# A new order of the seven products in a channel mixer's tiles, with PSUM banks of its own for the third product, on one NeuronCore

## The reference

```python
def causal_dwconv(u, prev, w, b):
    full = jnp.concatenate([prev, u], axis=1)
    return b + sum(full[:, i:i + L] * w[i] for i in range(3)), full[:, -2:]

def conv_glu(h, prev, w_in, conv_w, conv_b, w_out):
    g, u = jnp.split(h @ w_in, [2816], axis=-1)
    gc, new_prev = causal_dwconv(g, prev, conv_w, conv_b)
    return (jax.nn.gelu(gc, approximate=False) * u) @ w_out, new_prev
```

## Time and profile before

| | |
|---|---|
| median of 3 runs | 2664.94 us (2663.79 to 2665.84) |
| the profiled execution: time | 2669.07 us |
| its span in the trace | 2667.2 us |
| mean granted clock of TensorE | 0.991 |
| TensorE busy | 2586.1 us, 97% |
| VectorE busy | 1485.7 us, 56% |
| ScalarE busy | 1001.2 us, 38% |
| GpSimd busy | 991.4 us, 37% |
| DMA queues, share of 16 engines' span | 24.3% (SyncE's and ScalarE's loads and stores) |
| channel mixer of layer 0, tiles 1 to 21 | 599.2 to 1047.0 us |
| tile 1 of layer 1 | from 1954.9 us |

### The profile page before, as it was taken

One profiled execution on the slowest core, in us unless ns is written; L12 is line 12 of the kernel. 1 busy time (PEld: TensorE's weight loads), 2 busy tenths in 40 slices (PEclk: granted clock), 3 DMA queues, 4 the chain that ended last, 5 costly groups with the idle time before them and its releaser, 6 DMA issues.

```text
span 2667.2 us, 43368 instructions
## 1 busy us (share of the span) xinstructions
PE 2586.1 (97%) x18206; PEld 2502.4 (94%) x18206; DVE 1485.7 (56%) x2646; ACT 1001.2 (38%) x1651; POOL 991.4 (37%) x560
## 2 busy tenths in 40 slices
PE   8999999997999999999999989999979999999999
PEld 6899999997999999999998988889979999999999
DVE  6635353477545545555625875555685455545554
ACT  6333333363322332111437766444543323331111
POOL 5121212165443344443522223223373443444431
PEclk9999999998999999999999999999989999999999
DMA  3111111122222224222213354122112222233222
GB/s 109 34 36 34 36 38 36 35 97 65 87 73 81 80 81 178 80 97 97 70 40 119 116 193 134 51 88 73 60 62 89 73 80 73 88 117 134 97 97 99
DMA packets 182158, 221.93 MB, mean 83 GB/s; under 512 B 16689, under 2 KB 145343, under 8 KB 181327
## 3 DMA queue, kind: packets, MB, share of 16 engines
q1 hardware_dynamic: 179567, 217.08, 24.3%
q10 hardware_dynamic: 2400, 2.10, 0.3%
HBM read 160.56 MB, written 58.59 MB: 82 GB/s over the span
## 4 chain that ended last, share of the span: by engine, by line
PE 85%; DVE 9%; issue 2%; ACT 2%; DMA 1%; SPq 0%; POOL 0%; DVEq 0%; ACTq 0%; POOLq 0%
PE ps L341 13%; PE ps L343 13%; PE ps L342 13%; PE ps L751 10%; PE ps L753 10%; PE ps L752 10%; PE ps L2285 3%; PE ps L1214 1%; PE ps L2269 1%; PE ps L1201 1%; PE ps L1202 1%; PE ps L1203 1%; PE ps L1285 1%; DVE hflat L486 1%; DVE xT L585 1%
## 5 line engine op out<-in xcount | busy, mean ns | idle before, releaser
L585 DVE TENSOR_TENSOR xT<-xT,ps 128x352 f32<-128x352 f32 x672 | 347.2, 519 | 249.4 <-PE ps L343 248.2
L1084 POOL TENSOR_TENSOR wlo<-wraw,whi 128x1024 fp32r<-128x1024 f32 x84 | 211.4, 2516 | 475.4 <-DVE s_raw L963 475.4
L306 POOL TENSOR_TENSOR wlo<-wraw,whi 128x2048 fp32r<-128x2048 f32 (+1 forms) x37 | 168.4, 4552 | 500.8 <-ACT whi L299 471.4
L341 PE MATMUL ps<-fahi,whi 128*128 128x352 f32 x960 | 311.1, 324 | 0.1
L343 PE MATMUL ps<-fahi,wlo 128*128 128x352 f32 x960 | 308.3, 321 | 0.0
L342 PE MATMUL ps<-falo,whi 128*128 128x352 f32 x960 | 307.9, 321 | 0.0
L299 ACT ACTIVATE whi<-wraw 128x2048 fp32r<-128x2048 f32 x40 | 76.6, 1915 | 401.9 <-DMA wraw<-w_ffn_out 332.4
L341 PE MATMUL ps<-hh,whi 128*128 128x352 f32 x648 | 213.6, 330 | 0.6 <-ACT cqr L2598 0.3
L343 PE MATMUL ps<-hh,wlo 128*128 128x352 f32 x648 | 208.0, 321 | 0.0
L342 PE MATMUL ps<-hl,whi 128*128 128x352 f32 x648 | 207.8, 321 | 0.0
L753 PE MATMUL ps<-hh,wlo 128*128 128x264 f32 x672 | 191.2, 284 | 0.0
(11 more groups left out here) (411 smaller groups left out, 8061.4 us busy)
## 6 DMA issues: line engine op xcount, KB each, us to landing
wraw<-w_ffn_in SPq DMA_DIRECT2D x88, 512.0 KB, 3.8
s_a<-hf SPq DMA_DIRECT2D x44, 528.0 KB, 3.4
wraw<-w_ffn_out SPq DMA_DIRECT2D x44, 512.0 KB, 4.3
fa<-s_a SPq DMA_DIRECT2D x40, 528.0 KB, 6.1
wraw<-w_gla_in SPq DMA_DIRECT2D x24, 512.0 KB, 4.7
s_x<-xT SPq DMA_DIRECT2D x6, 1408.0 KB, 5.8
xback<-s_x SPq DMA_DIRECT2D x4, 2112.0 KB, 12.9
s_k<-kw SPq DMA_DIRECT2D x8, 784.0 KB, 3.3
```

Source lines behind the costliest of these rows:

```text
L306: pool.tensor_tensor(lo[:, 0:cols], raw[:, 0:cols], hi[:, 0:cols].bitcast(F32), ALU.subtract).then_inc(S("w_lo"), 1)
L341: nc.tensor.matmul(out, w[0], x[0], start=start, stop=False)
L585: dve.tensor_tensor(xT[:, m, tc(j)], xT[:, m, tc(j)], ps[:, banks[i % len(banks)], 0:TC], ALU.add)\
L1084: return pool.tensor_tensor(lo[:, cols], raw[:, cols], hi[:, cols].bitcast(F32), ALU.subtract)
```

## The change

The products run in the order P1, P2, P3, P6, P5, P7, P4. P3 (the product of X22) no longer gathers with P5 but has banks 2 and 3 (`U_EARLY`), and `gate_right` adds it to the right gate by an addition of its own, after the fifth product (P5). The convolution of a tile follows in that tile, ahead of `up_right` and `up_left`; `glu(f)` follows these. P4, in banks 0 and 1, is now the last product, so that the next tile's P2 waits for `up_left`. In the first two or three tiles the order is an own one. T1 and T3 are formed in another way from the same blocks. In tile 1 all low parts are made on VectorE; GpSimd starts with the extra weights of tile 2. Its three calls per tile are now `w_low_in`, `w_low_extra` (512 and 1024 columns) and `w_low_side`. On SyncE the second half of a tile's weights is loaded after the seventh product instead of the sixth, and in the last tile the reloads of the residual stream (`xback`) and of the first activations stand in another order.

```diff
-        U_SUM, U_DOWN, U_SIDE = 6, 0, 4
+        U_SUM, U_DOWN, U_SIDE, U_EARLY = 6, 0, 4, 2
+        ORDER = ("P1", "P2", "P3", "P6", "P5", "P7", "P4")
...
+            def p2():
+                if f == 1:
+                    pe.wait_ge(S("gate_taken"), 2 * layer + 1)
+                else:
+                    pe.wait_ge(S("summed"), nth("summed", 4 * u))
+                product(U_DOWN, w_in(1), x_part(HK, 0)).then_inc(S("prod"), 1)
...
+            def p3():
+                pe.wait_ge(S("s_lo"), nth("s_lo", 3 * u + 2))
+                if f == 1:
+                    pe.wait_ge(S("gate_taken"), 2 * layer + 2)
+                else:
+                    pe.wait_ge(S("summed"), nth("summed", 4 * u - 2))
+                product(U_EARLY, w_extra(2), x_part(HK, TH)).then_inc(S("prod"), 1)
...
act_ffn:
+            snap(1, 1)
+            w_hi_sums(2)
+            snap(1, 2)
+            for f in range(2, NF):
+                snap(f, 0)
+                if f < 4:
+                    gelu((0, 2)[f - 2])
...
                 snap(f, 1)
                 if f < NF - 1:
                     w_hi_sums(f + 1)
                 else:
                     a_high(0)
                 snap(f, 2)
-            gelu(NF - 1)
+                gelu(1 if f == 2 else f)
...
dve_ffn:
+            def up_left(f):
+                u, left = unit_no(layer, f), two_of(a_rows(f)[:, 0, :])
+                dve.wait_ge(S("prod"), nth("prod", 7 * u + ORDER.index("P4") + 1))
+                dve.wait_ge(S("summed"), nth("summed", 4 * u + 3))
+                dve.tensor_tensor(left, left, two(U_DOWN), ALU.add).then_inc(S("summed"), 1)
+            def gate_right(f):
+                u, v = unit_no(layer, f), two_of(fg[f % 2][:, 2 + TH:2 + T])
+                dve.wait_ge(S("snap"), nth("snap", 3 * u + 2))
+                dve.wait_ge(S("prod"), nth("prod", 7 * u + ORDER.index("P5") + 1))
+                dve.tensor_tensor(v, v, two(U_EARLY), ALU.add).then_inc(S("early"), 1)
+                dve.wait_ge(S("early"), nth("early", u + 1))
                 dve.tensor_tensor(v, v, two(U_SIDE), ALU.add).then_inc(S("summed"), 1)
...
             s_sums(1)
-            t_sums()
+            t_sum("T1")
+            t_sum("T2")
+            w_low_in(1)
+            w_low_extra(1)
+            t_sum("T3")
+            t_sum("T4")
             t_low("T2", 2)
+            w_low_side(1)
+            t_low("T1", 1)
+            t_low("T3", 3)
             gate_left(1)
-            conv(0)
             t_low("T4", 4)
             s_sums(2)
+            w_low_in(2)
+            gate_right(1)
+            up_right(1)
+            up_left(1)
+            conv(0)
+            gate_left(2)
+            s_sums(3)
             glu(0)
-            the_rest(1)
             conv(1)
-            for f in range(2, NF):
+            gate_right(2)
+            up_right(2)
+            glu(1)
+            up_left(2)
+            conv(2)
+            gate_left(3)
+            s_sums(4)
+            glu(2)
+            gate_right(3)
+            conv(3)
+            up_right(3)
+            up_left(3)
+            glu(3)
+            for f in range(4, NF):
                 gate_left(f)
-                glu(f - 1)
                 if f + 1 < NF:
                     s_sums(f + 1)
-                the_rest(f)
+                gate_right(f)
                 conv(f)
+                up_right(f)
+                up_left(f)
+                if f + 1 < NF:
+                    glu(f)
...
pool_ffn:
             norm_pool(pool, 1 + 2 * layer, m)
-            pool.wait_ge(S("w_lo"), c0 + 1)
-            w_low_in(1)
-            w_low_first(1)
-            w_low_side(1)
-            t_low("T1", 1)
-            w_low_last(1)
-            t_low("T3", 3)
+            pool.wait_ge(S("w_lo"), c0 + 3)
             for f in range(2, NF):
-                w_low_in(f)
-                w_low_first(f)
+                if f > 2:
+                    w_low_in(f)
+                w_low_extra(f)
                 w_low_side(f)
-                w_low_last(f)
```

More of the change, by code:

```diff
@@ L699, in sp_ffn @@
                     sp_unit_w(sp, layer, c0, f + 2, 0)
-                sp_a_out(sp, layer, f - 1)
-                prod(f, 6)
+                if f > 1:
+                    sp_a_out(sp, layer, f - 1 if f > 2 else 0)
+                prod(f, ORDER.index("P4") + 1)
                 if f + 2 < NF:
@@ L705, in sp_ffn @@
                     sp_w_out(sp, layer, c0, 0)
+                if f == 2:
+                    sp_a_out(sp, layer, 1)
             f = NF - 1
@@ L782, in pe_unit_ffn @@
[L782 to L792, removed]
@@ new lines, in p6, with p5 @@
+            def p6():
+                pe.wait_ge(S("s_lo"), nth("s_lo", 3 * u + 2))
+                pe.wait_ge(S("snap"), nth("snap", 3 * u + 1))
+                if f == 1:
+                    pe.wait_ge(S("t_lo_dve"), nth("t_lo_dve", 4 * layer + 1))
+                product(U_SUM, w_extra(0), t_part("T2"), True).then_inc(S("prod"), 1)
+            def p5():
+                pe.wait_ge(S("s_lo"), nth("s_lo", 3 * u + 3))
+                if f == 1:
+                    pe.wait_ge(S("t_lo_dve"), nth("t_lo_dve", 4 * layer + 2))
+                else:
+                    pe.wait_ge(S("summed"), nth("summed", 4 * u - 1))
+                product(U_SIDE, w_in(2), t_part("T1")).then_inc(S("prod"), 1)
@@ new lines, in p7, with p4 @@
+            def p7():
+                pe.wait_ge(S("s_lo"), nth("s_lo", 3 * u + 3))
+                pe.wait_ge(S("snap"), nth("snap", 3 * u + 2))
+                if f == 1:
+                    pe.wait_ge(S("t_lo_dve"), nth("t_lo_dve", 4 * layer + 3))
+                product(U_SUM, w_extra(1), t_part("T3"), True).then_inc(S("prod"), 1)
+            def p4():
+                pe.wait_ge(S("summed"), nth("summed", 4 * u + 1))
+                if f == 1:
+                    pe.wait_ge(S("t_lo_dve"), nth("t_lo_dve", 4 * layer + 4))
+                product(U_DOWN, w_in(3), t_part("T4")).then_inc(S("prod"), 1)
@@ new lines, in p3 @@
+            def p3():
+                pe.wait_ge(S("s_lo"), nth("s_lo", 3 * u + 2))
+                if f == 1:
+                    pe.wait_ge(S("gate_taken"), 2 * layer + 2)
+                else:
+                    pe.wait_ge(S("summed"), nth("summed", 4 * u - 2))
+                product(U_EARLY, w_extra(2), x_part(HK, TH)).then_inc(S("prod"), 1)
+            products = {"P1": p1, "P2": p2, "P3": p3, "P4": p4, "P5": p5, "P6": p6, "P7": p7}
+            for name in ORDER:
+                products[name]()
@@ L963, in s_sums, with t_sum @@
                 dve.tensor_tensor(s4, w[1], s2, ALU.subtract).then_inc(S("s_sum"), 1)
[L965 to L977, removed]
+            def t_sum(name):
+                x11, x21, x12, x22 = [t_raw[n] for n in ("T3", "T4", "T1", "T2")]
+                if name == "T1":
+                    dve.wait_ge(S("h32"), KD * NCH * (m + 1))
+                    dve.wait_ge(S("h_hi"), KD * NCH * (m + 1))
+                    dve.wait_ge(S("h_lo"), POOL_LO * NCH * (m + 1))
+                    dve.tensor_tensor(x12, x12, x11, ALU.subtract).then_inc(S("t_sum"), 1)
+                elif name == "T2":
+                    dve.wait_ge(S("t_sum"), nth("t_sum", 4 * layer + 1))
+                    dve.tensor_tensor(x22, x22, x12, ALU.subtract).then_inc(S("t_sum"), 1)
+                elif name == "T3":
+                    dve.wait_ge(S("t_sum"), nth("t_sum", 4 * layer + 2))
+                    dve.tensor_tensor(x11, x22, x11, ALU.subtract).then_inc(S("t_sum"), 1)
+                else:
+                    dve.wait_ge(S("t_sum"), nth("t_sum", 4 * layer + 2))
+                    dve.tensor_tensor(x21, x21, x22, ALU.subtract).then_inc(S("t_sum"), 1)
             def t_low(name, n):
@@ L982, in t_low, with low, w_low_in, w_low_extra @@
                                   ALU.subtract).then_inc(S("t_lo_dve"), 1)
+            def low(lo, raw, hi, cols):
+                return dve.tensor_tensor(lo[:, cols], raw[:, cols], hi[:, cols].bitcast(F32), ALU.subtract)
+            def w_low_in(f):
+                slot, n, _, _ = chunk(c0 + f)
+                dve.wait_ge(S("w_hi"), n + 1)
+                dve.wait_ge(S("s_sum"), nth("s_sum", 4 * unit_no(layer, f) + 4))
+                low(wlo[slot], wraw[slot], whi[slot], slice(0, 2 * QB)).then_inc(S("w_lo"), 1)
+            def w_low_extra(f):
+                dve.wait_ge(S("s_hi"), nth("s_hi", 2 * unit_no(layer, f) + 1))
+                low(s_lo[f % 2], s_raw[f % 2], s_hi[f % 2], slice(0, 3 * QB)).then_inc(S("s_lo"), 2)
+            def w_low_side(f):
+                slot = chunk(c0 + f)[0]
+                dve.wait_ge(S("s_hi"), nth("s_hi", 2 * unit_no(layer, f) + 2))
+                low(wlo[slot], wraw[slot], whi[slot], slice(2 * QB, 4 * QB)).then_inc(S("s_lo"), 1)
             def gate_left(f):
@@ L1033, in glu @@
                     dve.wait_ge(S("gate_taken"), 2 * layer + 2)
+                else:
```

(1 more changed line is left out.)

96 lines of the change are left out of this document (34 added, 62 removed).

## The result

| | before | after |
|---|---|---|
| median of the runs compared | 2665.39 us | 2712.93 us (2712.79 to 2714.07) |
| ratio after / before | | 1.0177, interval 1.0161 to 1.0193 |
| profiled execution: time, span | 2669.07, 2667.2 us | 2712.93, 2711.1 us |
| granted clock, mean | 0.991 | 0.994 |
| VectorE busy | 1485.7 us | 1644.7 us |

The change makes the kernel 1.8% slower; 2712 was forecast.

A forecast was written before the change was run, and what follows sets the result against it. TensorE, busy 97%, was taken as the bound. Per layer 15.6 us won in tile 1, less 5.8, 2 and 31.5 lost, gives 23.7 us slower, twice: 47 us, forecast 2712 us, 8-in-10 range 2694 to 2742.

The forecast's parts named there:

- What bounds the kernel and what could be won: TensorE, 97% busy; tile 1 loses 19.1 us a layer, of which the new first tile wins 15.6.
- Turns between VectorE and GpSimd: VectorE operations with SBUF inputs and GpSimd's never run together; queued, they alternate by instruction; additions reading PSUM do not wait.
- Settled tiles: Tiles 4 to 21: product 2 waits for up_left behind the convolution, 1.75 us each, 18 times, 31.5 us a layer.
- the first of the two cases: Settled tiles: the 32-column copy takes the turn, GpSimd's side weights follow, then the convolution; stall 1.86 us a tile.
- the other case: Settled tiles: the copy needs no turn, the convolution's step one takes it; stall 1.66 us a tile.
- Tiles 2 and 3: GpSimd's pieces alternate with the convolutions; tile 3's product 2 waits 5.8 us for up_left, plus 2 us of lower clock.
- The clock term: After tile 3's long stall TensorE runs at the lower clock, counted as 2 us a layer.
- What costs nothing: Third product's banks, later load of the second weight half, reordered last-tile input: free; the last bounded at 0 to 2 us a layer.
- The sum: Per layer +15.6 - 5.8 - 2 - 31.5 = -23.7 us, twice: 47 us slower, median 2712.
- The rivals: Slack absorbs the convolution (chance 0.11), clock falls with each stall (0.08), half the convolutions escape, 2680 (0.04).
- the clock did not fall in settled tiles: Rival: clock falls with each stall, 61 us more, 2773, or 2732 if a third do; chance 0.08.
- The first rival: Settled tiles: side weights stay out from between convolution steps, up_left done at 19.9 us, no stall: 2637; chance 0.11.

The follow-up runs named there:

- experiment 2: Changed kernel, but in tiles 4 to 21 ScalarE copies raw weights instead of GpSimd computing low parts of extra and side weights: 2652.60 us, 0.9947 of before.
- experiment 1: Changed kernel with the convolution, its gelu and glu behind the last addition (up_left) in tiles 4 to 21: 2654.76 us, 0.9960 of before.
- experiment 3: Changed kernel with the high parts of extra and side weights ahead of the second snapshot in ScalarE's queue: 2658.27 us, 0.9965 of before.
- (6): From experiment 5, tile 1's weight low parts, T1's and T3's low parts and w_low_in(2) back on GpSimd: 2658.57 us, 0.9970 of before.
- Experiment 4: Changed kernel with the copy of 32 columns moved from ahead of the convolution's first step to behind its second: 2709.54 us, 1.0161 of before.
- experiment 5: On experiment 1's order: convolution behind the last addition in all tiles from 1, tile 1's last snapshot ahead of tile 2's high parts: 2638.30 us, 0.9895 of before.
- experiment 8: From experiment 5, tile 1's last snapshot again behind tile 2's high parts on ScalarE: 2639.48 us, 0.9898 of before.

## Why the prediction was right

- **What bounds the kernel and what could be won.** Right: tile 1 gave 17.0 us of the 19.1 in layer 0 and 16.8 in layer 1 (15.6 forecast). Of the 1.4 more, 0.4 is a chain from the first T sum to tile 2 of 28.8 us instead of 29.2, and 1.0 comes from ahead of it: VectorE began its T sums 6.3 us before TensorE's tile 1 (592.99 and 599.30) and not 5.3 as before.
- **Turns between VectorE and GpSimd.** Shown by runs and not only by reading: in settled tiles the stall went with GpSimd's pieces left out (experiment 2), with VectorE's work moved out of their way (1) and with one collision instead of two (3), and splitting the first tile over both engines cost 20 us (6).
- **Settled tiles.** 1.66 or 1.86 us of stall were forecast, 1.75 taken; 1.72 measured, by the first of the two cases, whose sum of 1.86 was 0.14 too long: the copy did take the turn, 1.28 us instead of 0.18. In this the trace agrees with what the Trainium skill (SBUF — State Buffer, "Who interferes with whom") says of copies. Experiment 4 shows the other case, 0.14 us shorter in idle time and 0.10 in the tile, where the prediction had 0.2.
- **Tiles 2 and 3.** 5.8 us forecast, 5.0 measured, as 3.3 us of stall and 1.8 at the lower clock. The mechanism was right in kind, the count of turns was not: see the last section. The clock term, 2 us, was 2.6 in layer 0 and 1.5 in layer 1, behind the 3.3 us stall of tile 3. The lower clock in tile 2, after the 1.91 us wait, which the prediction had as a wait without a fall, cost nothing more: in experiment 1 the clock stayed at 1.00 there, and the stretch took 28.28 us with a stall of 4.70 instead of 28.35 with one of 3.25. VectorE's chain sets its end either way.
- **What costs nothing.** The later weight load: settled tiles have no wait for it. The reordered reloads of the last tile, bound 0 to 2 us a layer: TensorE has no wait for them. But the later load costs 0.7 us a layer behind the last tile, which the prediction has no term for. There it brings `w_out`: issued at 1044.25 before, ahead of the tile's end at 1047.0, and at 1068.93 after, behind its end at 1068.7. ScalarE could use it 12.5 us after the issue in both:

```profile
1056.71 1.92 ACT L299 ACTIVATE whi<-wraw 128x2048 fp32r<-128x2048 f32 x1 [3.79 <-DMA wraw<-w_ffn_out]
```

```profile
1081.46 1.92 ACT L299 ACTIVATE whi<-wraw 128x2048 fp32r<-128x2048 f32 x1 [9.10 <-DMA wraw<-w_ffn_out]
```

  GpSimd's low part of these weights and, behind it, that of the second group of activations (`falo`) follow, and TensorE waits for the latter.
- **The sum.** 23.7 us a layer forecast, 21.6 and 20.7 in the trace; 47 in all, against 43.9 between the profiled executions and 47.5 between the medians. That the forecast met the median to 1 us is luck in part: its sum was 2.1 us too slow in layer 0 (1.4 in tile 1, 0.8 in tiles 2 and 3, 0.5 in settled tiles, less 0.6 of clock) and 3.0 in layer 1, and the medians lie 3.6 us further apart than the profiled executions.
- **The rivals.** The slack did not absorb the convolution, and the clock did not fall in settled tiles (granted 1.00 over 17 stalls of 1.48 us). The first rival's 2637, for a kernel in which no collision costs anything, is where experiment 5 came out (2638), with another order; experiments 1 and 2, in which only the collisions of settled tiles are gone, took 2655 and 2653.

## What to carry to other kernels

Before moving elementwise work between queues, lay the timelines of VectorE and GpSimd beside each other: in these traces a VectorE operation with all its inputs in SBUF and a GpSimd subtraction cost the sum of their times, while VectorE's additions that also read PSUM kept their 0.70 us. The slack must hold the rest of the piece that is running, plus a whole piece for each further one that GpSimd has queued when VectorE's next such instruction comes: none in experiment 3, one in the changed kernel's settled tiles, more in its tile 2. The convolution's place was free on VectorE's own timeline and not on GpSimd's. If a stage waits for both engines, give the whole chain of pieces to one of them, and put behind the last urgent addition what nobody waits for.

## What the runs showed of the hardware that had not been expected

That the turn is taken by the instruction, however short. In tile 2 the changed kernel's VectorE rows read (the last of them two copies of 2 columns, 256 values each):

```profile
634.94 2.39 DVE L1072 COPY sm<-fg 128x32 f32<-128x32 f32 x1
637.25 0.82 DVE L1076 TENSOR_SCALAR fc<-fg,par 128x1056 f32<-128x1056 f32 x1
638.10 2.19 DVE L1079 SCALAR_TENSOR_TENSOR fc<-fg,par,fc 128x1024 f32<-128x1024 f32 x1
640.21 2.38 DVE L1081 SCALAR_TENSOR_TENSOR fc<-sm,par,fc 128x32 f32<-128x32 f32 x1
642.52 2.47 DVE L1085 COPY csv<-fg 128x2 f32<-128x2 f32 x2
```

A multiply-add over 32 columns took 2.38 us against 0.25 in a settled tile of the same trace, and the copies of 2 columns 2.47 against 0.23. The prediction let the convolution's short instructions pass free.

The other point is the clock, for which the rows give no rule. TensorE idles 1.9 us ahead of tile 2 in both layers of six of these kernels (the changed one and experiments 1, 2, 3, 4 and 8). Behind five of these twelve waits the granted clock fell to 0.50, 1.2 GHz, for a while: in both layers of the changed kernel and of experiment 8 and in layer 1 of experiment 4. Behind the other seven it stayed at 1.00. The 4 us behind the same wait in layer 0 of experiment 1 and of the changed kernel:

```profile
620.36:624.36 4.00, 4.00 (x33) 4.00 (x34) 3.86 (x4) 0.00 (x0) 4.00 (x2) 1.00 0.32 97
```

```profile
621.79:625.79 4.00, 4.00 (x20) 4.00 (x21) 3.86 (x4) 0.00 (x0) 4.00 (x2) 0.57 0.33 100
```

What decides between them no run here shows. Behind the 34 waits of 1.47 or 1.48 us ahead of settled tiles it never fell.
